# Attention steps of a pair of heads rearranged: values in front of the scores two pairs on, transposes two steps later

## The reference, cut to what matters

```
h = rms_norm(x, norm1_g)
q, k, v, z = jnp.split(einsum('bsd,de->bse', h, w_in1), 4, axis=-1)
q = rms_norm(to_heads(q), q_norm_g) * (HEAD_DIM ** -0.5)
k = rms_norm(to_heads(k), k_norm_g)
s = q . k - slope_of_head * (query position - key position), causal
o = softmax(s) @ v
x = x + (o * silu(z)) @ w_out1
```

## Time and profile before

| | |
|---|---|
| median of 3 runs | 339.28 us (339.14 to 340.86) |
| the profiled execution | 339.02 us |
| its span, first to last instruction | 337.2 us |
| PE busy | 328.9 us (98%) |
| DVE busy | 266.7 us (79%) |
| ACT busy | 225.2 us (67%) |
| granted TensorE clock, mean | 0.999 |

### The profile page before, as it was taken

How to read it: one execution, slowest core, us unless ns; L and a number is a source line. 1 busy time by engine, 2 the same in 40 slices (tenths; PEclk the granted TensorE clock), 3 DMA queues, 4 the chain that set the end, 5 groups by cost and what they waited for, 6 DMA issues and landing times.

```text
span 337.2 us, 5723 instructions
## 1 busy us (share of the span) xinstructions
PE 328.9 (98%) x2196; PEld 298.0 (88%) x2196; DVE 266.7 (79%) x493; ACT 225.2 (67%) x425; POOL 41.0 (12%) x50
## 2 busy tenths in 40 slices
PE   8999999999999999999989999999999999999995
PEld 8899999999889999989989999988887777688885
DVE  3998989899989999989777799755557686748633
ACT  5756876959799995149876466744647676675530
POOL 0000011223242101100200000005320040500000
PEclk9999999999999999999999999999999999999999
DMA  7987037798999858946869424591634323300003
GB/s 280 398 348 273 4 111 203 254 231 226 273 207 271 251 148 326 223 127 262 188 185 330 185 68 183 183 376 66 224 152 128 130 118 127 124 0 2 2 1 124
DMA packets 11691, 61.63 MB, mean 183 GB/s; under 512 B 1296, under 2 KB 1424, under 8 KB 5392
## 3 DMA queue, kind: packets, MB, share of 16 engines
q1 hardware_dynamic: 8064, 53.78, 44.2%
q0 software_dynamic: 3456, 7.34, 12.4%
q10 hardware_dynamic: 144, 0.15, 0.2%
HBM read 52.88 MB, written 1.05 MB: 160 GB/s over the span
## 4 chain that ended last, share of the span: by engine, by line
PE 63%; DVE 18%; ACT 9%; DMA 6%; issue 2%; SPq 0%; ACTq 0%
PE bank L1000 17%; PE bank L1002 16%; PE bank L1001 16%; DVE w_lo L672 6%; DVE scratch L785 4%; PE bank L1034 4%; DVE scratch L790 4%; DMA w_lo<-raw 3%; DMA raw<-w 3%; PE bank L1060 2%; PE bank L1218 2%; ACT w_hi L411 2%; PE bank L1245 2%; ACT scratch L494 2%; PE bank L1231 2%
## 5 line engine op out<-in xcount | busy, mean ns | idle before, releaser
L672 DVE TENSOR_TENSOR w_lo<-raw,w_hi 128x1024 fp32r<-128x1024 f32 x76 | 90.1, 1220 | 15.8 <-ACT w_hi L411 15.5
L411 ACT CAST w_hi<-raw 128x1024 fp32r<-128x1024 f32 x80 | 80.2, 1047 | 5.5 <-PE bank L1002 2.8
L1000 PE MATMUL bank<-h_hi,w_hi 128*128 128x256 f32 x208 | 59.6, 287 | 0.6 <-DVE w_lo L672 0.6
L1001 PE MATMUL bank<-h_lo,w_hi 128*128 128x256 f32 x208 | 58.8, 283 | 0.0
L1002 PE MATMUL bank<-h_hi,w_lo 128*128 128x256 f32 x208 | 58.8, 283 | 0.0
L1034 PE MATMUL bank<-H,raw 128*128 128x256 f32 x256 | 56.8, 379 | 1.2 <-DMA raw<-w 1.2
L1034 PEld LDWEIGHTS bank<-H,raw 128*128 128x128 f32 x256 | 48.0, 190 | 7.6 <-DMA raw<-w 1.4
L785 DVE SCALAR_TENSOR_TENSOR scratch<-scratch,params 128x256 f32<-128x256 f32 x114 | 47.0, 479 | 4.4 <-ACT scratch L507 4.3
L1000 PE MATMUL bank<-ya_hi,w_hi 128*128 128x256 f32 x160 | 47.3, 296 | 0.0
L1002 PE MATMUL bank<-ya_hi,w_lo 128*128 128x256 f32 x160 | 45.2, 282 | 0.0
L1001 PE MATMUL bank<-ya_lo,w_hi 128*128 128x256 f32 x160 | 45.2, 282 | 0.0
(11 more groups left out here) (102 smaller groups left out, 546.3 us busy)
## 6 DMA issues: line engine op xcount, KB each, us to landing
raw<-w SPq DMA_DIRECT2D x49, 1024.0 KB, 5.0
side_v<-side_ring POOLq DMA_DIRECT2D x20, 256.0 KB, 5.1
w_lo<-raw POOLq DMA_DIRECT2D x4, 512.0 KB, 7.7
X<-xT SPq DMA_DIRECT2D x2, 512.0 KB, 5.0
out<-X SPq DMA_DIRECT2D x4, 256.0 KB, 2.7
consts<-const SPq DMA_DIRECT2D x1, 290.0 KB, 13.3
params<-vec ACTq DMA_DIRECT2D x1, 149.0 KB, 4.8
```

The source lines that it names most:

```text
L411: nc.scalar.copy(halves(w_hi, cut_slot(n), half), halves(raw, n % RAW, half)).then_inc(hi_cut, 1)
L672: nc.vector.tensor_tensor(halves(w_lo, cut_slot(n), half), halves(raw, n % RAW, half), halves(w_hi, cut_slot(n), half).bitcast(F32), ALU.s ...
L1000: nc.tensor.matmul(dst, wh, ah, start=start, stop=False, skip_group_check=True)
L1001: nc.tensor.matmul(dst, wh, al, start=False, stop=False, skip_group_check=True)
```

## The change

Two things change: the table of steps, and the turn, which is now issued at t itself on PE and ACT where it was at t + 1. DVE's code is the same, but it reads the same table, so its gates and low parts move with the values.

```diff
 def pair_steps(octet):
-    gap, to_turn, to_values, first = PAIR_TIMES[octet]
-    scores = [gap * i + first + octet * VAL_STEP for i in range(4)]
-    return scores, [s + to_turn for s in scores], [s + to_values for s in scores]
-
-PAIR_TIMES = (8, 7, 11, 3), (6, 6, 10, 13)
-VAL_STEP = 32
+    return PAIR_STEPS[octet]
+
+PAIR_STEPS = (((3, 11, 19, 27), (13, 21, 29, 37), (19, 27, 35, 45)),
+              ((45, 51, 57, 63), (53, 59, 65, 70), (57, 63, 68, 73)))
@@ ACT
-                        if s == turns[i] + 1:
+                        if s == turns[i]:
                             pair_turn_out(4 * octet + i)
```

## The result

The changed kernel takes 347.63 us (median of 6 runs, 345.36 to 348.54) against 339.29 us, a ratio of 1.0233 with an interval of 1.0204 to 1.0262: slower by 2.3%. The sign was as forecast, the size was not: 344.5 was forecast with a range up to 346.8. The profiled run, 345.36 us with a span of 343.6, is the fastest of the six, and the only one whose mean granted clock is 1.00. Two runs at 0.995 took 346.6 and 346.9, three at 0.990 took 348.4 to 348.5. So the loss has two parts: 6 us that are in this profile, and 1 to 3 us more that only the other five runs have.

What follows compares the result with a forecast made beforehand. PE was taken to bound the kernel, busy 98% of the span. Savings of 0.55 and 0.8 against waits summed to +5.25 on 339.02, giving 344.3 us profiled, 344.5 as median, with a range of 343.0 to 346.2.

Steps and rivals of the forecast that it cites:

- rival C: More than summed: clock falls to 1.2 GHz behind the 2.8 us wait, five slow steps, +3.4, about 348 us; chance 0.10.
- the wait of step 37: Turn of pair 3 on PE waits for DVE's gate of pair 2, behind the subtraction of step 34: +2.8 us.
- the gates: DVE gates pair n too late for PE's next turn, now 2 steps after the values, before 5; waits paid in full.
- step 21: Turn of pair 1 on PE waits for DVE's gate of pair 0: +2.0 us, bounds 0.95 and 2.6.
- step 29: Turn of pair 2 on PE waits for the bank ACT is copying and the gate of pair 1: +0.4 us.
- step 32: Turn of keys on PE waits for the turn-out of step 29, queued behind two pieces of ACT's work: +0.2 us.
- step 50: PE waits for the values' copies of step 47 on ACT, 0.3 later than PE: +0.2 us.
- step 59: PE's turn waits for the gate of pair 4, behind subtractions of steps 55 and 56 and a bias: +0.9 us.
- steps 65 and 68: Waits on PE in octet 1 of under 0.1 us each, together +0.1 us.
- The merged block: Values directly before scores at steps 19, 27, 45, 57, 63: 0.11 saved each, -0.55 us, bounds 0 and -1.0.
- Rival A: Not slower: gates start by 271.4 and 290.2, no new wait at steps 21 and 37, about 338.0 us; chance 0.08.
- Rival B: Half the waits: ACT catches up, 0.95 at step 21, some 1.2 at 37; +1.7, 341.2 us; chance 0.15.

Runs made afterwards that it cites:

- both delays removed: Changed kernel with four instead of two buffers for the probabilities and DVE's subtraction of steps 18 and 34 moved behind the gate: 338.81 us, ratio 0.9986.
- the best kernel: Changed kernel with four probability buffers, subtractions moved behind the gates, turns placed by the gates, second key turn at step 33: 337.4 us, ratio 0.9946.
- The run with four buffers: Changed kernel with four buffers for the probabilities instead of two, so exponentials no longer wait for the previous pair's turn: 342.04 us, ratio 1.0082.

## Why the prediction was right and wrong

**Wrong: rival C, the clock.** The text gave it one in ten, because the longest wait of 2.8 seemed too short, and named as its price five slow steps, +3.4. By their mean clock it happened in ten of the eleven timed runs of this kernel. The mechanism and the place are those of rival C, behind the wait of step 37; the one fall that a profile shows lasted two steps and cost 1.5 us, not 3.4. The step that failed is this: the sum prices the wait of step 37 by its length alone and puts the clock behind it at nothing, although the rows said nothing about a wait of that length. The runs showed 1.5 to 1.6 us for the fall behind it. With the waits filled by matmuls the kernel takes 345.0, inside the forecast's own range; with them idle 347.6 and 346.8 in the two sets of runs. That the first median lies clearly above the range comes from the runs at a mean clock of 0.990, which lose 1.7 us more at a place that no profile shows; that part of the cause stays open. The 348 of rival C is near some of the runs by luck, as its price for one fall is twice what was measured. In the Trainium skill, TensorE: Matmul & The Clock Gate (HAM oscillation) has idle gaps above this one as its condition; that does not hold here, where 2.7 us were enough in most runs. The measurement decides.

**Right: the gates.** The three places, the engine, the line and the order of the causes came out as said. Wait by wait, forecast against measured at full clock: step 21 2.0 and 2.21; step 29 0.4 and 0.44; step 32 0.2 and 0.36; step 37 2.8 and 2.70; step 50 0.2 and 0.30 more than before; step 59 0.9 and 1.10; steps 65 and 68 0.1 and 0.52. The gate of pair 0 was forecast at 273.40 and began at 273.84, of which 0.40 is a later start of the whole stage in that run. ACT's cast of step 15 was forecast at 267.14 and, less the same 0.40, began at 267.20.

**Mis-sized, small.** All waits but that of step 37 came out longer than forecast; over all of them it is 1.0 us, most of it at steps 59, 65 and 68. The merged block saves 0.20 and not 0.11: the term was 1.0, its outer bound, instead of 0.55. The text had counted at least three changeovers for the merged block; the timeline shows two, 0.09 going in and 0.11 coming out, and none between 64 columns and 64 rows. The two errors partly cancel, which is luck. With both the sum is +5.8 instead of +5.25; the run at full clock took 345.36 where 344.3 was forecast for a profiled one, of which 0.6 are these terms and 0.4 the later start of the stage.

**Rival A**, that the gates come in time, is wrong for the kernel as changed: the gates that were to start by 271.4 and 290.2 began at 273.84 and 293.51. It is right as a description of what the kernel could be: with both delays removed the change gains 0.4 us, with turns moved as well 1.8. Of the range given for that case (337.5 to 338.0) the best kernel lies just below.

**Rival B**, that ACT catches up, is out by the first profile, where the waits have their full length. The run with four buffers takes most of ACT's lateness away (its cast of step 15 is 0.33 late instead of 1.26, both counted from the first scores), and 1.28 and 1.91 remain, where B had 0.95 and 1.2 with none of it.

## What to carry to other kernels

When a piece of work moves in one queue, find who must answer it in another queue and what stands ahead of the answer there; here 0.4 us of gate was 3.6 us late behind a sum and a subtraction, and the subtraction could go behind it without a new wait on PE. Swap that order before giving up the move: the same table of steps is 8 us slower or 0.4 us faster by it and two more buffers. And price a long wait on TensorE twice, once for its length and once for the clock behind it, which may only show in runs other than the profiled one: compare the profiled run's time and clock with the median first.

## What the runs showed of the hardware

- With an idle time of 2.54 us on PE (2.7 by the ledger), in a stretch that was busy on both sides, the granted clock fell to its lower level: one profile shows the place, and the mean clock and the time say so for five of six runs with that idle time and none at step 21. With 2.05 us (2.2) alone it fell in none of four, and not with 1.75 us (1.9) in the one profile that has it. In the profile it fell near the end of the idle time and was back at 1.00 about two steps later, at a cost of 1.5 us.
- Going from a block with 64 output columns straight to one with 64 rows costs no pause of its own: 0.80 us from the start of the values to what follows, whether that is the scores or a matmul on the full array. Transposes on the full array with the scores directly behind them cost as much as the two blocks apart (1.71 against 0.66 + 1.05 us, in the kernel before).
